# Wide identity matmuls of constants between the head pairs and solve steps of the RWKV sample tokens

## The reference

```python
def step(S, inp):
    r_t, w_t, k_t, v_t, a_t, b_t = inp
    sa = jnp.einsum('bhvk,bhk->bhv', S, a_t)
    S = S * w_t[:, :, None, :] + sa[..., None] * b_t[:, :, None, :] + v_t[..., None] * k_t[:, :, None, :]
    return S, jnp.einsum('bhvk,bhk->bhv', S, r_t)
S, o = lax.scan(step, S0.astype(f32), seq)
```

## Time and profile before

| | us |
|---|---|
| median of 3 runs | 3062.38 |
| lowest, highest | 3061.59, 3069.55 |
| span of the profiled execution | 3063.8 |
| TensorE matmul busy in it | 2927.4 |
| DVE, ACT, POOL busy in it | 1681.3, 1175.6, 258.4 |
| mean granted TensorE clock in it | 0.962 |

### The profile page before, as it was taken

How to read it: one execution, slowest core, us unless ns; L and a number is a source line. 1 busy time by engine, 2 the same in 40 slices (tenths; PEclk the granted TensorE clock), 3 DMA queues, 4 the chain that set the end, 5 groups by cost and what they waited for, 6 DMA issues and landing times.

```text
span 3063.8 us, 64641 instructions
## 1 busy us (share of the span) xinstructions
PE 2927.4 (96%) x28861; PEld 2729.0 (89%) x28861; DVE 1681.3 (55%) x2501; ACT 1175.6 (38%) x1748; POOL 258.4 (8%) x343
## 2 busy tenths in 40 slices
PE   8998999999999997999999899999999899999998
PEld 7996788799999985899999888799999876887997
DVE  5646443566565546665564673456566456445654
ACT  4433222344444423543443543144344342224432
POOL 1010001200000102000000111400000100021001
PEclk9999999799999998999999899899999999998998
DMA  8442401154554654344644332264554424012541
GB/s 256 141 148 101 140 30 32 42 182 130 188 163 139 234 174 183 123 155 148 192 139 150 116 135 64 68 187 139 181 169 135 154 98 137 3 34 71 178 131 63
DMA packets 333705, 402.36 MB, mean 131 GB/s; under 512 B 14778, under 2 KB 287567, under 8 KB 333069
## 3 DMA queue, kind: packets, MB, share of 16 engines
q1 hardware_dynamic: 320912, 355.99, 35.7%
q0 software_dynamic: 12592, 43.45, 4.8%
HBM read 384.83 MB, written 14.57 MB: 130 GB/s over the span
## 4 chain that ended last, share of the span: by engine, by line
PE 90%; DVE 5%; ACT 2%; issue 1%; DMA 1%; POOL 0%; SPq 0%; ACTq 0%; DVEq 0%; POOLq 0%
PE banks L882 22%; PE banks L884 21%; PE banks L883 21%; PE banks L915 2%; PE banks L1194 2%; PE banks L1030 2%; PE banks L973 1%; PE banks L995 1%; PE banks L1173 1%; PE banks L1147 1%; PE banks L1278 1%; ACT work L2042 1%; PE banks L1236 1%; PE banks L1129 1%; DVE h L2382 1%
## 5 line engine op out<-in xcount | busy, mean ns | idle before, releaser
L882 PE MATMUL banks<-h_hi,w_hi 128*128 128x288 f32 x2816 | 837.8, 298 | 7.1 <-DVE h_lo L2389 6.6
L2397 DVE TENSOR_TENSOR w_lo<-ring,w_hi 128x2048 fp32r<-128x2048 f32 (+1 forms) x304 | 611.3, 2011 | 412.2 <-ACT w_hi L1966 412.1
L883 PE MATMUL banks<-h_hi,w_lo 128*128 128x288 f32 x2816 | 831.7, 295 | 0.0
L884 PE MATMUL banks<-h_lo,w_hi 128*128 128x288 f32 x2816 | 828.8, 294 | 0.0
L1966 ACT CAST w_hi<-ring 128x2048 fp32r<-128x2048 f32 (+1 forms) x304 | 511.4, 1683 | 591.2 <-PE banks L884 555.9
L882 PEld LDWEIGHTS banks<-h_hi,w_hi 128*128 128x128 f32 x2816 | 528.4, 188 | 10.4 <-issue 5.9
L884 PEld LDWEIGHTS banks<-h_lo,w_hi 128*128 128x128 f32 x2816 | 531.3, 189 | 0.0
L883 PEld LDWEIGHTS banks<-h_hi,w_lo 128*128 128x128 f32 x2816 | 529.6, 188 | 0.4
L882 PE MATMUL banks<-hid_hi,w_hi 128*128 128x288 f32 x1408 | 416.1, 296 | 0.0
L883 PE MATMUL banks<-hid_hi,w_lo 128*128 128x288 f32 x1408 | 415.4, 295 | 0.0
L884 PE MATMUL banks<-hid_lo,w_hi 128*128 128x288 f32 x1408 | 414.3, 294 | 0.0
(11 more groups left out here) (573 smaller groups left out, 4452.8 us busy)
## 6 DMA issues: line engine op xcount, KB each, us to landing
ring<-in_ffn_w_gate SPq DMA_DIRECT2D x88, 1024.0 KB, 5.5
ring<-in_ffn_w_up SPq DMA_DIRECT2D x88, 1024.0 KB, 8.0
ring<-in_ffn_w_down SPq DMA_DIRECT2D x64, 768.0 KB, 4.5
ring<-in_ffn_w_down SPq DMA_DIRECT2D x64, 640.0 KB, 5.7
ring<-in_rwkv_w_rkv SPq DMA_DIRECT2D x24, 1024.0 KB, 7.3
ring<-in_gdn_w_in SPq DMA_DIRECT2D x16, 1024.0 KB, 6.6
ring<-in_attn_w_qkv SPq DMA_DIRECT2D x12, 1024.0 KB, 7.3
ring<-in_rwkv_w_o SPq DMA_DIRECT2D x8, 1024.0 KB, 6.3
```

Of the source, the lines that this page charges most:

```text
L882: nc.tensor.matmul(out, w_hi_k, x_hi_k, start=start, stop=False)
L883: nc.tensor.matmul(out, w_lo_k, x_hi_k, start=False, stop=False)
L884: return nc.tensor.matmul(out, w_hi_k, x_lo_k, start=False, stop=stop)
L2397: nc.vector.tensor_tensor(w_lo[e][:, 0:k, :], raw, w_hi[e][:, 0:k, :], ALU.subtract).then_inc(w_lo_ready, 1)
```

## The change

A helper `keep_clock(at, n=1)` is added, which issues n multiplications of `ident` by `consts[:, 0:256]`, 128 rows by 256 columns in f32, into bank `at`. Nothing reads what they write. It is called with `at` 2 and n 1 in `sample_solve`: behind each head pair of the read (seven of these before the matmul that raises the semaphore, the eighth behind it), and behind each of the four calls of `over_heads`. That is 12 in each RWKV layer and 24 in all. They wait for nothing and signal nothing.

```diff
@@ block.tensor
             after = follow(pe)
 
+            def keep_clock(at, n=1):
+
+                for _ in range(n):
+                    nc.tensor.matmul(bank[at][:, 0:256], ident, consts[:, 0:256], start=True, stop=True)
+
@@ sample_solve
                                                     start=True, stop=True)
+                    if hp < CH - 1:
+                        keep_clock(2)
                 last.then_inc(seq_st_raw, 1)
+                keep_clock(2)
@@
                 after(seq_st_ready)
                 over_heads(5, ((seqAST, ident_heads), (seqA, seqV)), seq_rhs_raw, final=False)
+                keep_clock(2)
                 after(seq_rhs_ready)
                 over_heads(1, ((solve0, seqR),), seq_w_raw)
+                keep_clock(2)
                 after(seq_w_ready)
                 over_heads(5, ((solve1, seqW),), seq_rhs_raw, first=False)
+                keep_clock(2)
                 after(seq_rhs_ready)
                 over_heads(3, ((solve0, seqR),), seq_u_raw)
+                keep_clock(2)
                 after(seq_uv_ready)
```

## The result

The changed kernel takes 3076.19 us (median of 7 runs, 3074.09 to 3086.19), the kernel before in the same session 3065.03 us (3058.00 to 3073.62). The ratio is 1.0043, 95% interval 1.0024 to 1.0062: slower by 0.4%, clear of no change. The forecast was 3075. Five of the seven executions took 3074 to 3077 us, at a mean granted clock of 0.963 or 0.964, and two took 3086 us, at 0.959 and 0.960; only one of the five was profiled, so what the clock did in the two is not known.

The account below looks back on a forecast made before the run. TensorE was taken to bound the kernel. Layer 0 (9.6 + 0.4 - 0.6 - 2.5 - 2.4 = +4.5) and layer 3 (9.6 + 0.4 - 0.6 - 1.4 = +8.0) gave +12.5 us: 3075 us, range 3057 to 3082.

Parts of the forecast that it names:

- The bound: TensorE, busy 90% of the 3063.8 us span: time given to or taken from read and solve moves everything behind.
- The insertion's price: One wide multiplication between 64x64 ones costs 0.74 us at full clock and 1.37 at half.
- The rival of a cheap insertion: Clock falls in the read, but only columns count, 0.86 us an insertion at half clock: 3067 us; chance 0.10.
- The clock in the read: Read with insertions stays too thin (32% at full clock), so the clock falls early in both layers.
- the first rival: The clock holds throughout the read in both layers: sum -9.0 us, 3053 us; chance 0.19.
- The sum: Read, wait, first call, later calls and part behind: layer 0 +4.5 us, layer 3 +8.0, together +12.5.
- the wait behind them: Wait between read and solve: the eighth insertion outlasts it, +0.4 us in each layer.
- Calls in layer 0: Solve's later calls in layer 0 every 1.83 us instead of 2.66, -2.5 us; layer 3 nothing.
- the part behind: From L1303 to L1086, behind the solve's calls, at full clock: -2.4 us in layer 0, -1.4 in layer 3.
- The first call: Solve's first call: clock back by its end, in part inside it, -0.6 us in each layer.
- The third rival: The clock does not come back in the solve: +11.2 us layer 0, +14.7 layer 3, 3088 us; chance 0.06.

Follow-up runs that it names:

- the doubled variant: Against the changed kernel, two wide multiplications instead of one behind each head pair of the read; median 3082.70 us, ratio to before 1.0055.
- 320 tiled columns: Against the changed kernel, each insertion as two 64x64 multiplications of 320 columns, one more pair ahead of the read; 3056.71 us, repeated 3056.31.
- 256 tiled columns: Against the changed kernel, each insertion as two 64x64 multiplications of 256 columns; 3066.87 us; with one more pair ahead of the read 3065.99.

## Why the prediction was right

**The bound.** What the two stretches gained came through to the span: +12.0 us in them, +10.7 in all. The rest is 1.3 us shorter, less than it varies between profiled executions.

**The insertion's price.** Forecast 0.74 us at full clock from 16-row records; measured 0.73 in layer 3 of the change (1.66 us from the first head pair to the second, less 0.93), and 0.73 in the doubled variant (2.09 a head pair for two, less 0.93 and 0.43). At half clock forecast 1.37, measured 2.96 - 1.71 = 1.25: the ratio of 1.85, taken from other records, was a little high, since the columns take twice as long at half clock (0.43 and 0.85) but what goes with the change of tile does not (0.30 and 0.40). The rival of a cheap insertion falls: at 0.86 us it had the wait behind the read and the tile at nothing. The Trainium skill's page "TensorEngine Tiling (Array Packing)", Key Properties, says that a change of tiling mode drains TensorE; the trace agrees that such a change costs, 0.30 and 0.40 us with its weight load. By the 262 cycles, 0.11 us, that the Trainium skill's page "TensorE: Matmul & The Clock Gate", Back-to-back issue gap, gives for 256 columns the reads would hardly have moved; the trace has 0.73 us for this f32 multiplication.

**The clock in the read.** It fell in both layers, so the first rival falls. The forecast's reason, that too little of the read moves columns over the whole height of the array, fits the variants: with two wide multiplications behind a head pair the clock held in one of two layers, with 320 tiled columns in both, twice, and with 256 tiled columns it fell in both, twice. All of these vary the columns; that the height counts was tested by the 16 rows alone, and in the solve, since in the read the clock falls with 128 rows as well. What the forecast did not have is that the stream which holds the clock in one layer may leave it at half in the other.

**The sum.** The reads grew by 8.6 and 8.9 us from first to last start (forecast 9.6 each; to 21.3 us in layer 0, where about 22 was named), the wait behind them by 0.35 (0.4). Calls in layer 0 gave 2.5 (2.5), the part behind 2.6 in layer 0 (2.4). The first call was mis-sized in layer 3: forecast -0.6, measured +0.3, since the clock came back behind it and its insertion still ran mostly at half (start to start of the first two calls 4.62 us, before 4.34); in layer 0 it was -0.4. Behind the solve layer 3 gave 1.0 instead of 1.4: one group of 16 records (L1335) took 1.62 us where its twin takes 1.05. No wait for another engine is shown; the weight loads stand still for 0.39 us in it, and the cause was not tested. The errors went both ways and nearly cancel: layer 0 +3.4 us for +4.5, layer 3 +8.6 for +8.0, together +12.0 in the stretches for +12.5.

**Where it was luck.** The forecast stood on the median of three executions, 3062.38; that of seven in the session of the result was 3065.03, so +12.6 us were forecast and +11.2 came, and the two misses bring 3075 as near to 3076.19 as it is. The sum also takes from one execution which layer's solve had the clock before; the others were not profiled. The third rival, that the clock does not come back in the solve (3088 us), falls for the profiled execution; for the two that took 3086 us it can't be excluded.

## What to carry to other kernels

Filler matmuls can pay where the engine waits anyway: ahead of the solve's waits they cost almost nothing (0.35 us where one outlasted its wait at half clock) and the clock came back earlier (0.2 to 0.3% of the kernel here), while the same filler in an unbroken stream cost 1.25 us each at half clock. If filler must stand in a stream, give it the tile shape of its neighbours (0.43 instead of 0.73 us), and read from the trace whether the clock then holds, for filler behind which the clock falls all the same is paid at half clock for nothing. Before adding it, price one insertion from rows with the same operand type and a change of tile, not from its columns alone.

## What the runs showed of the hardware

A multiplication of 16 rows by 256 columns and one of 128 rows by 256 columns take the same time (1.22 us for both records at half clock), but in the profiled executions only the latter brought the granted clock back in the solve: with 16 rows PE was busy without a gap for 34.13 us at 0.5. The same instruction stream held the full clock through one layer's read and stayed at half through the other's (2.09 and 3.81 us a head pair in one execution); in the second the clock had fallen 1.3 us in. And 320 instead of 256 columns, 0.10 us more in 1.37, was the difference between losing the clock in all four profiled reads and holding it in all four.
